# A streaming encoder step on one core: transposed input, norm applied after the first products, split weight loads, queries in pieces of 272 columns

## The reference, cut to what matters

```python
h = rmsnorm(x, norm_mix)                       # x * rsqrt(mean(x*x) + EPS) * gain
z = h @ w_in                                   # sections q | k | v | g | a | b, 512 columns each
u = a * sigmoid(b)                             # GLU, then a depthwise convolution of 31 taps over tokens
y = concat([silu(g) * groupnorm(retention(q, k, v)), silu(layernorm(conv(u)))]) @ w_out
x = x + y
h = rmsnorm(x, norm_ffn)
scores = (h @ peer_query) . peer_sub_keys      # 8 heads, 2 x 128 keys each, top 16 of each, top 16 of the sums
out = sum_e gate_e * gelu(h . peer_down[e]) * peer_up[e]     # 8 * 16 experts for each token
y = rmsnorm(x + out, norm_final)
```

## Time and profile before

| | us |
|---|---|
| median of three runs | 1677.19 |
| lowest, highest | 1674.56, 1678.44 |
| the profiled execution | 1672.85 |
| its span in the trace | 1671.1 |
| PE busy in the span | 1419.8 (85%) |
| DVE busy | 1178.5 (71%) |
| POOL busy | 729.8 (44%) |
| ACT busy | 504.4 (30%) |
| the 16 DMA engines: mean rate over the span | 363 GB/s |

### The profile page before, as it was taken

The page is one execution under the profiler, slowest core; times in us unless marked ns, Lnnn a source line. Parts: engine busy times, 40 slices in busy tenths (PEclk is TensorE's granted clock), DMA queues, the critical chain, the costliest instruction groups (busy, mean ns, idle before and its releaser), DMA issues.

```text
span 1671.1 us, 14832 instructions
## 1 busy us (share of the span) xinstructions
PE 1419.8 (85%) x4373; PEld 685.7 (41%) x4373; DVE 1178.5 (71%) x2555; ACT 504.4 (30%) x1607; POOL 729.8 (44%) x623
## 2 busy tenths in 40 slices
PE   7999999899798789788987898789878987767843
PEld 6744465555344334333433343334333433322311
DVE  2897858875876777677767776677777777767755
ACT  2111212432333333233333333333333333333332
POOL 1003714454444454454445454444544444454452
PEclk9999999999899999899999998899999999999876
DMA  6202307999999999999999999999999999999997
GB/s 238 101 1 65 143 30 298 365 421 421 421 421 421 421 422 420 421 422 421 406 423 421 420 406 422 421 421 414 420 422 384 413 422 421 421 422 421 422 421 293
DMA packets 85328, 606.22 MB, mean 363 GB/s; under 512 B 11008, under 2 KB 11520, under 8 KB 13568
## 3 DMA queue, kind: packets, MB, share of 16 engines
q0 software_dynamic: 78336, 570.46, 82.5%
q1 hardware_dynamic: 6912, 34.81, 5.6%
HBM read 601.97 MB, written 2.88 MB: 362 GB/s over the span
## 4 chain that ended last, share of the span: by engine, by line
PE 40%; DMA 33%; DVE 14%; issue 4%; DVEq 3%; POOL 3%; ACT 3%; ACTq 0%; POOLq 0%; SPq 0%
DMA arena<-experts,expert 32%; PE ps L1546 25%; PE ps L1504 6%; DVE arena L1201 5%; PE ps L1407 4%; DVE region_b L942 3%; DVEq L1085 3%; POOL arena L550 2%; PE ps L1395 2%; PE ps L1476 1%; ACT weight L788 1%; PE ps L1384 1%; ACT late L799 1%; DVE cst L1181 0%; DVE cst L1178 0%
## 5 line engine op out<-in xcount | busy, mean ns | idle before, releaser
L1546 PE MATMUL ps<-arena,late 128*128 128x512 f32 x2016 | 960.9, 634 | 179.0 <-ACT late L799 178.8
L550 POOL DMA_INDIRECT arena<-experts,expert x544 | 659.6, 1212 | 724.3 <-PE ps L1546 599.2
L1201 DVE CUSTOM_DVE_ANT_0 arena<-arena,hn 128x1024 f32<-128x1024 f32 x544 | 655.1, 1223 | 357.8 <-DMA arena<-experts,expert 351.1
L1546 PEld LDWEIGHTS ps<-arena,late 128*128 128x128 f32 x2016 | 400.9, 203 | 721.7 <-issue 560.0
L785 ACT ACTIVATE gl<-dots 128x4 f32<-128x4 f32 (+1 forms) x139 | 28.5, 205 | 800.9 <-DVE dots L1201 800.8
L799 ACT ACTIVATE late<-cst,weight 128x128 f32<-128x128 f32 (+1 forms) x536 | 169.1, 385 | 9.7 <-issue 0.3
L788 ACT ACTIVATE weight<-gl,gate 128x1 f32<-128x1 f32 x544 | 116.0, 283 | 9.5
L1407 PE MATMUL ps<-arena,hT 128*128 128x512 f32 x256 | 111.7, 595 | 0.0
L1504 PE MATMUL ps<-hT,region_b 128*128 128x512 f32 x224 | 98.4, 592 | 0.0
L942 DVE SCALAR_TENSOR_TENSOR region_b<-region_b,par 128x574 f32<-128x574 f32 x120 | 92.5, 813 | 4.9 <-issue 0.4
L1407 PEld LDWEIGHTS ps<-arena,hT 128*128 128x128 f32 x256 | 48.6, 192 | 58.5 <-issue 58.4
(11 more groups left out here) (156 smaller groups left out, 863.4 us busy)
## 6 DMA issues: line engine op xcount, KB each, us to landing
arena<-weights SPq DMA_DIRECT2D x8, 2048.0 KB, 11.6
region_b<-head_weights SPq DMA_DIRECT2D x8, 1152.0 KB, 9.5
arena<-experts,expert POOLq DMA_INDIRECT x544
xs<-x_prompt SPq DMA_DIRECT2D x4, 512.0 KB, 5.6
y_prompt<-xs SPq DMA_DIRECT2D x4, 512.0 KB, 4.3
cst<-consts SPq DMA_DIRECT2D x1, 836.0 KB, 21.7
hn<-gain_ffn SPq DMA_DIRECT2D x1, 512.0 KB, 3.9
region_b<-gain_ffn SPq DMA_DIRECT2D x1, 512.0 KB, 3.7
```

The lines of the kernel that those rows point to most:

```text
L550: pool.indirect_dma_start(rows_of(n), None, experts, bass.IndirectOffsetOnAxis(ap=expert[:, vt % BUFS, k:k + 1], axis=0))\
L1201: last = v.tensor_tensor_reduce(out=rows_of(n)[:, 0:D], in0=rows_of(n)[:, 0:D], in1=hn[:, tile_of(vt)], scale=1.0, scalar=0.0, op0=ALU.mul ...
L1546: last = mm(ps[:, 2 * (vt % 2) + half, :], diag[:, n % DIAGS, :], rows_of(n)[:, D + half * SEC:D + (half + 1) * SEC], start=k == first * G ...
```

## The change

The host lays the input out a second time, transposed (`x_turned`, two halves of 272 tokens), and sections A and B by channel block. SP loads in this order: parameters, first half of `x_turned`, block 0 of A, second half, block 1 of A, the identity, the five tiles of x, blocks 0 and 1 of B, the two states, the rest of A, the rest of B, section Q, the constants.

DVE multiplies the gain of each feature into `hT` in place, 16 instructions of 272 columns. PE needs no transposes: it makes the parts (A, 0), (A, 1), (B, 0) from unnormed columns (`RAW`). The sums of squares and POOL's roots stay; ACT writes each tile's roots on a diagonal, PE spreads them over all partitions by a product with ones (`spread`, two banks between A1 and B0), ACT copies the result to `row_scale`. DVE then makes normed columns for all k (`norm_columns`, 16 instructions), and scales the three raw parts after their eviction; Tanh of block B0 is a separate ACT instruction. ACT copies the normed columns back into `hT` (`normed_back`, four instructions) for Q, K, V, G.

The queries: the 32 sample tokens of head 0 go with tile 3 (160 columns). For heads 1 to 7 there are four pieces of 272 columns (key set by token half), behind groups 0 to 3 of the first unit. For head 1 they stand before the four groups of unit 2, on PE and on ACT alike, and the scores after the unit's last group.

```diff
-    order = turn("norm_t", 0) + turn("norm_t", 1) + turn("norm_t", 2) + glu(S_A, (0, 0), (1, 0)) + turn("norm_t", 3)
-    order += turn("norm_t", SAMPLE) + glu(S_A, (0, 1), (1, 1)) + glu(S_B, (0, 0), (0, 1), (1, 0), (1, 1))
+    early = [(c, i) for c in (0, 1) for i in range(2)]
+    order = glu(S_A, *early) + [("spread", 0), ("spread", 1)] + glu(S_B, *early)
...
-    return order + query(3) + sums(1, 0) + keys(3) + query(4) + sums(1, 1) + keys(4) + sums(1, 2) + sums(1, 3)
+    return order + query(3) + sums(1, 0) + keys(3) + sums(1, 1) + keys(4) + sums(1, 2) + sums(1, 3)
...
-            x_rows(0)
+            sp.dma_start(par[:, :], params).then_inc(s_par, 16)
+            turned_columns(0)
+            glu_weights(S_A, 0, 1, s_lead[S_A, 0])
+            turned_columns(1)
+            glu_weights(S_A, 1, 2, s_lead[S_A, 1])
             sp.dma_start(cst[:, C_IDENT:], consts[:, C_IDENT:]).then_inc(s_ident, 16)
...
+            for t in range(TILES):
+                x_rows(t)
+            glu_weights(S_B, 0, 1, s_lead[S_B, 0])
+            glu_weights(S_B, 1, 2, s_lead[S_B, 1])
...
+            glu_weights(S_A, 2, CT, s_w[0])
+            glu_weights(S_B, 2, CT, s_w[1])
+            weight_rows(S_Q)
...
+            def first_tanh():
+                act.wait_ge(s_scaled, 1)
+                nc.scalar.activation(conv[:, 0, :], conv[:, 0, :], ACT.Tanh).then_inc(s_tanh, 1)
+
+            def normed_back():
+
+                for k in range(0, KD, 2):
+                    nc.scalar.activation(hT[:, k:k + 2, :], normedT[:, k:k + 2, :], ACT.Copy).then_inc(s_back, 1)
...
             softmax(3)
+            later_query(1, 0)
             group(2, 0)
-            later_query(1, 0)
+            later_query(1, 1)
             group(2, 1)
-            later_query(1, 1)
+            later_query(1, 2)
             group(2, 2)
-            later_query(1, 2)
+            later_query(1, 3)
             group(2, 3)
...
-                    return {0: {1: lambda: later_query(head + 1, 0), 3: lambda: later_query(head + 1, 1)},
-                            1: {1: lambda: later_query(head + 1, 2), 3: lambda: later_scores(head + 1)}}.get(m, {})
+                    return {0: {g + 1: lambda g=g: later_query(head + 1, g) for g in range(3)},
+                            1: {0: lambda: later_query(head + 1, 3), 3: lambda: later_scores(head + 1)}}.get(m, {})
...
+            for i in range(2):
+                dve.wait_ge(s_xt[i], 16)
+                for k in range(KD):
+                    half = hT[:, k, i * HALF:(i + 1) * HALF]
+                    v.tensor_scalar(out=half, in0=half, scalar1=par[:, G_MIX + k:G_MIX + k + 1], scalar2=None,
+                                    op0=ALU.mult).then_inc(s_gained, 1)
...
             def glu_part(s, c, i):
...
                 for k in range(KD):
+                    if (s, c) == (S_A, 0):
+                        pe.wait_ge(s_gained, i * KD + k + 1)
+                    elif (s, c, i) == (S_B, 1, 0):
+                        pe.wait_ge(s_normed, k + 1)
...
+            def spread(i):
+                out = open_bank(("spread", i))
+                for t in [SAMPLE] if i else range(SAMPLE):
+                    r, lo = ROWS[t], 0 if i else t * P
+                    pe.wait_ge(s_root, t + 1)
+                    last = mm(out[:, lo:lo + r], ones[0:r, :], root_diag[0:r, t, 0:r], start=True, stop=True)
                 done(last)
...
             later_query(1, 2)
             sum_up(2, 2)
+            later_query(1, 3)
+            sum_up(2, 3)
             later_scores(1)
-            sum_up(2, 3)
             head_tile(3, {})
```

More of the change, by code:

```diff
@@ L246, in build @@
         first_gain = hn[:, 1]
+        hn_flat = hn[:, :, :].rearrange("p t d -> p (t d)")
+        normedT = hn_flat[:, 0:KD * T].rearrange("p (k t) -> p k t", k=KD)
+        row_scale = hn_flat[:, KD * T:KD * T + WIDE]
+        root_diag = z[:, :, S_V, 0:P]
+        ones = z[:, 0, S_G, 0:P]
         channel_sum = scratch[:, 4 * RW:4 * RW + WIDE]
@@ L339, in build @@
         s_ident = sem("s_ident")
+        s_xt = [sem(f"s_xt{i}") for i in range(2)]
+        s_lead = {(s, c): sem(f"s_lead{s}_{c}") for s in (S_A, S_B) for c in range(2)}
+        s_gained = sem("s_gained")
+        s_root = sem("s_root")
+        s_scaled = sem("s_scaled")
+        s_tanh = sem("s_tanh")
+        s_normed = sem("s_normed")
+        s_back = sem("s_back")
         s_cst = sem("s_cst")
@@ L390, in build, with flat @@
         s_yout = sem("s_yout")
+        def flat(section):
+            return section.rearrange("p k n -> p (k n)")
         def slot_filled(n):
@@ L620, in _ @@
                 act.wait_ge(s_x[t], 16)
-                square_sum(xs[0:ROWS[t], t], t, ROWS[t], hn[0:ROWS[t], t])
+                square_sum(xs[0:ROWS[t], t], t, ROWS[t], z[0:ROWS[t], t, S_Q:S_K + 1].rearrange("p s n -> p (s n)"))
+            act.wait_ge(s_ident, 16)
+            for t in range(TILES):
+                r = ROWS[t]
+                act.wait_ge(s_rstd, t + 1)
+                nc.scalar.activation(root_diag[0:r, t, 0:r], ident[0:r, 0:r], ACT.Copy, scale=rstd[0:r, t:t + 1])\
+                    .then_inc(s_root, 1)
+            def spread(i):
+                name = ("spread", i)
+                filled(name)
+                lo, n = (SEQ + PAD, DEC) if i else (0, SEQ)
+                emptied(name, nc.scalar.activation(row_scale[:, lo:lo + n], bank(name)[:, 0:n], ACT.Copy))
             def glu_part(s, c, i):
                 name = ("glu", s, c, i)
-                func = ACT.Copy if s == S_A else ACT.Tanh
+                func = ACT.Tanh if s == S_B and (s, c) not in RAW else ACT.Copy
                 to = u[:, c, PAD:EXT] if s == S_A else conv[:, c, :]
@@ L897, in filled @@
                 dve.wait_ge(s_pe, JOB[name] + 1)
+            v.memset(ones[:, :], 1.0)
+            v.memset(row_scale[:, SEQ:SEQ + PAD], 1.0)
             v.memset(ones_cw[:, :], 1.0 / CW)
@@ new lines, in _, with norm_columns @@
+            v.tensor_scalar(out=half_ln[:, :], in0=par[:, G_LNG:G_TAPS], scalar1=0.5, scalar2=None, op0=ALU.mult)
+            dve.wait_ge(s_by["act"], EMPTIED[("spread", 1)])
+            def norm_columns(k):
+                v.tensor_tensor(out=normedT[:, k, 0:SEQ], in0=hT[:, k, 0:SEQ], in1=row_scale[:, 0:SEQ], op=ALU.mult)
+                v.tensor_tensor(out=normedT[:, k, SEQ:T], in0=hT[:, k, SEQ:T], in1=row_scale[:, SEQ + PAD:], op=ALU.mult)                    .then_inc(s_normed, 1)
+            for k in range(KD):
+                norm_columns(k)
@@ L1475, in first_query @@
                     for k in range(KD):
[L1476 to L1477 removed]
+                        last = mm(out[:, s * width:(s + 1) * width], head_w[0][0][:, k, s * KEYS:(s + 1) * KEYS],
+                                  hT[:, k, t * P:t * P + width], start=k == 0, stop=k == KD - 1)
                 done(last)
             def first_scores(t):
[L1481 removed]
+                pe.wait_ge(s_by["act"], EMPTIED[("query", min(t, HT - 1))])
                 out = open_bank(("scores", t))
@@ L1642, in lay_out @@
     weights = w_all.reshape(KD, P, SECTIONS, SEC).transpose(2, 1, 0, 3)
+    weights = np.array(weights)
+    for s in (S_A, S_B):
+        weights[s] = weights[s].reshape(P, KD, CT, P).transpose(0, 2, 1, 3).reshape(P, KD, SEC)
+    x_turned = np.concatenate([a["x_prompt"][0], a["x_sample"][0]]).reshape(2, HALF, KD, P).transpose(0, 3, 2, 1)
     queries = a["peer_query"][0].reshape(KD, P, PH, 2 * KEYS).transpose(2, 1, 0, 3).reshape(PH, P, HEAD_W)
```

179 lines of the change are left out of this document (88 added, 91 removed).

## The result

The changed kernel takes 1682.65 us (median of 15 runs, 1678.02 to 1686.81), the kernel before 1676.19 us beside it (15 runs, 1673.65 to 1680.07). The ratio is 1.0039, 95% interval 1.0029 to 1.0050: **slower by 6.5 us**, where 1670.6 was forecast and nothing above 1675.5 stood in the range. The profiled execution of the changed kernel took 1678.52 us, at the low end of its own runs; its span is 1676.7 against 1671.1.

The account below looks back on a forecast made before the run. The prediction took PE's GLU parts and DVE's taps to gate the time before the gathers, then the DMA queue alone. Start 6.6 us sooner, queries 0, unit 2 0: median 1677.19 to 1670.6, range 1665.0 to 1675.5.

Parts of the forecast that it names:

- The start: Up to ACT taking up part (B, 1, 1): at 40.4 us instead of 46.99, 6.6 us sooner, carried to the end.
- first data 7.7: Start: first weights and columns there at 7.7 us, bounds 5.9 and 8.6.
- half pace 2.0: Start: PE's slow first stretch now falls on part (A, 0, 0) and costs 2.0 us, bounds 0 and 3.5.
- eight parts and spreads: Start: eight GLU parts on PE take 29.5 us, the two spreads' ten PE rows 1.2 us.
- The first gather: End of the start: issued near 238.7 us, against 245.27 before.
- the covers named there: Start: seven side works, among them second half of `x_turned`, gains, roots, normed columns and loads, that must stay covered.
- The queries in steady heads: Heads 1 to 7: 2.5 us of PE less per head, beside a DMA queue that never emptied; value 0.
- rival 3: Dips in the DMA rate are real: 4.3 us at head 7, half of all recovered; 1666.3, to 1664. Chance 0.10.
- Unit 2: ACT waits for each piece before its group, rounds 12.4 us against 9.94 of data; price 0, bounds 0 and 3.
- the cushion of 7 us: Gathers' issue to landing, 14.86 and 13.28 us, less one gather (2.5) and smallest load (3.3): some 7 us spare.
- rival 1: Unit 2 breaks the cushion a little: DMAs pause by 3 us around 440 to 500; 1673.6. Chance 0.14.
- Rival 2: Slower: unit 2 starves the gathers, decided once PE is over 7 us further behind than before. Chance 0.07.

Follow-up runs that it names:

- act_order: The changed kernel with ACT in unit 2 taking group (2, g) ahead of piece (1, g), as before; PE's order stays as changed. 1670.62 us, ratio 0.9965.
- warm_start: act_order with 56 matmuls of ones on ones, 128 columns each, on PE ahead of its first part. 1676.22 us, ratio 0.9999.
- front_alone: The new start with everything about the queries as in the kernel before. 1670.62 us, ratio 0.9963 against the kernel before.
- queries_alone: Start, loads and normalisation of the kernel before, with pieces, orders and scores of the changed kernel. 1687.02 us, ratio 1.0064.
- scores_early: The changed kernel with PE making head 1's scores ahead of sum (2, 3), as before; ACT's order stays as changed. 1678.28 us, ratio 1.0002.
- clock_kept_7: The changed kernel with 7 unused matmuls of 128 columns on PE behind each of unit 2's four pieces. 1678.33 us, ratio 1.0015.
- warm_start_22: act_order with 22 matmuls of ones on ones, 128 columns each, on PE ahead of its first part. 1669.17 us, ratio 0.9958.
- clock_kept: The changed kernel with 30 unused matmuls of 128 columns on PE behind each of unit 2's four pieces. 1694.25 us, ratio 1.0109.

## Why the prediction was wrong, by its own steps

**The start: right.** Sum 40.4 for the taking up of (B, 1, 1), measured 41.34. Of its terms, first data 7.7 came at 8.56 (DVE had the columns at 7.30; the rest was the first weights of A, for which PE waits until 8.41 in act_order); half pace 2.0 was 1.8 (16.65 - 14.83, the four parts at full pace in warm_start; 2.9 in act_order); eight parts and spreads as put. The first gather, forecast near 238.7, came at 240.44. Carried to the end: 6.2 us by front_alone's ratio, against 6.6. None of the covers named there failed; the roots and `row_scale` did not hold PE between 25.05 and 33.8.

**The queries in steady heads: right.** Worth 0. The changed kernel's window with head 7's queries shows 420 GB/s where the earlier trace rows has 391. Its four pieces stand between 1283.5 and 1318.9 us. The 24 gathers ahead of them, read off the dot products, take 1273.51 - 1212.87 = 60.64 us and the 24 across them 1334.04 - 1273.51 = 60.53, against 60.60 and 60.66:

```profile
1273.51 1.23 DVE L1270 CUSTOM_DVE_ANT_0 arena<-arena,hn 128x1024 f32<-128x1024 f32 x1 [1.26 <-DMA arena<-experts,expert]
...
1334.04 1.22 DVE L1270 CUSTOM_DVE_ANT_0 arena<-arena,hn 128x1024 f32<-128x1024 f32 x1 [1.23 <-DMA arena<-experts,expert]
```

The dip was no loss, and filling it no gain; rival 3 falls with act_order equal to front_alone.

**Unit 2: the step that failed**, "Price: nothing while the cushion of 7 us holds. I take 0, bounds 0 and 3". The mechanism was seen (ACT waits for each piece ahead of the group, rounds of 12.4 us), and both of its sizes were wrong.

- *How late.* The prediction had ACT's copy of head 1's scores at about 415 on the clock of before, 3.5 to 4.5 us late, since PE "starts the unit nearly level". Its own round says otherwise. The first piece was copied at 372.0 before; three rounds of 12.4 are 37.2, then 1.9 to the diagonal, 6.87 for the sum and 0.9 for the first scores: 418.9, which is 8.1 late. A lag that is said to end "about as far behind as before" was never added up. Measured, on the clock of before: 420.06 + 5.65 = 425.7, so 14.9 late. The further 6.8 are 2.2 of a late first piece (368.57 + 5.65 against 371.99), 1.7 of a slow sum, 1.3 for ACT's gelu table, which in the old order was loaded at 360.57, ahead of 6.79 us of waiting for the dot products, and now stands behind the piece, 1.1 for rounds of 12.8, and 0.5 left over. The shift by 5.65 is itself generous: the last dot product ahead of group (2, 0) ends at 364.1 against 368.6, only 4.5 sooner, so some 1 us of the lateness was there when the unit's data arrived.
- *The late first piece* has its cause in something that the prediction booked as a help: with the sample's query gone from unit 1, PE had nothing in front of its last sum, idled 5.60 us and did that sum in 9.59 us, at a granted clock of 0.74. In front_alone, where the query is back, the same sum waits 0.63 us and takes 7.13. Gained work time became a gap and then slow matmuls. act_order has the same gap (5.59 us, then a sum of 9.93) and loses nothing by it.
- *The cushion.* "Some 7 us to spare" was the time in the DMA queue (13.28 and 14.86 us issue to landing) less one gather and one load. It measures about 3, counted from act_order. A queue's depth is not slack when the same late engine also holds up the next issue: a gather is issued only after the sum 12 slots back, and POOL's wait of 7.81 us on L1631 shows it.

The failed step, in its own terms, is thus a lateness put at 4.5 us at most that came out at 10.5 against act_order and 14.9 on the clock of before, and a cushion put at 7 us of which about 3 was there; the price put at 0, at most 3, measured 12.4 (1.0039 against 0.9965). 14.9 less 3 is 11.9 and looks like that price, but it mixes two starting points, and 10.5 less 3 gives the 7.3 us between two profiled executions; the medians lie further apart. The agreement is in part luck. How much of the 12.4 us goes through late slots and how much through DVE's late start on unit 3 stays open.

One sum of the range was off as well: rival 1's 3 us on the late bound of 4.2 gives 1676.0, not 1675.5. The measured time lies above both.

**The rivals.** Rival 1 had the right mechanism and place, capped at 3 us. Rival 2 had the sign, and its condition ("decides once PE is over 7 us further behind") with a cushion of 3 was met. The runs put about 4 of the 12 us on the clock: gaps of 2 us with some 11 us of work between were followed by sums at 8.83 in four of eight cases, and the slowest sum of unit 2 took 10.03 us for 7.13 (queries_alone). Together they had a chance of 0.21, too little for a step whose only defence was an estimated cushion. The view that was to show it, a DMA share under 1 between 420 and 500 us, did, and already from 395 us on.

## What to carry to other kernels

Where two engines serve each other from lists in program order, put first in each list what is ready first. An entry that waits for the other engine, put ahead of one whose data are there, turns overlap into turns, and a round then takes the sum of both engines' work (here 12.8 us, the changed kernel) instead of that of the busier one (10.5, act_order). Before calling a lag harmless, add up the rounds to the end of the stage and set them against a cushion that was measured, by one deliberate hold, not read off a queue's depth.

## What the runs showed of the hardware that was not expected

- Behind gaps of 1.97 or 1.98 us between bursts of 11 us on PE, four of eight sums of unit 2 took 8.83 us instead of 7.13, and behind gaps of 3.48 or 3.49 us they took 7.11, 8.80 or 10.03. With the gap filled down to 0.41 us none of three did, in the one profile there is. A gap is not needed: behind 3.65 us of 32-column products without any idle, a sum took 8.81 us in the kernel before and in front_alone. The granted clock goes with the sum's time in every row (read from the sum's start to that of the next instruction):

| run | sum at | gap before it | sum | granted clock |
|---|---|---|---|---|
| changed kernel | 384.76 | 1.97 | 7.13 | 1.00 |
| changed kernel | 397.53 | 1.97 | 8.83 | 0.80 |
| changed kernel | 412.00 | 1.97 | 7.13 | 1.00 |
| queries_alone | 391.71 | 1.98 | 8.83 | 0.80 |
| queries_alone | 406.19 | 1.98 | 7.13 | 1.00 |
| queries_alone | 418.97 | 1.98 | 8.83 | 0.80 |
| scores_early | 389.49 | 1.97 | 8.83 | 0.80 |
| scores_early | 403.95 | 1.97 | 7.13 | 1.00 |
| changed kernel | 372.02 | 3.49 | 7.11 | 1.00 |
| scores_early | 375.05 | 3.48 | 8.80 | 0.80 |
| queries_alone | 376.05 | 3.49 | 10.03 | 0.70 |
| clock_kept_7 | 385.94, 398.71, 411.49 | 0.41 | 7.13 each | 1.00 |
| kernel before | 395.88 | none | 8.81 | 0.80 |
| front_alone | 393.81 | none | 8.81 | 0.80 |

- PE's slow pace at the start was ended ahead of the data: 44 PE rows from 1.49 us on took 6.74 us (warm_start_22), and the first four parts then took 14.99 instead of the 17.71 us of act_order. In warm_start 18 rows fill the 3.90 us from 1.50 to 5.40, 0.22 us a row, and the last 62 of its 112 take 6.9 us, 0.11 a row. The column of the granted clock reads 1.00 from 1.50 to 5.40 and from 5.40 to 8.00 us alike, so it is the time of a row that shows this.
- A matmul of 128 columns on these 4-byte operands left two PE rows of 0.112 us (clock_kept); a fill of 30, expected to take 1.6 us, took 6.7.
